# Branch B of the attention computed with v as the weights and its result left transposed

## The reference

```python
sc = jnp.einsum('bqhd,bqkd->bhqk', q_blk, k_g).astype(jnp.float32) * scale
dist = jnp.abs(t[None, :, None] - top_idx).astype(jnp.float32)
sc = sc - slopes[None, :, None, None] * dist[:, None]
sc = jnp.where(valid[:, None], sc, -jnp.inf)
p = jax.nn.softmax(sc, axis=-1)
return jnp.einsum('bhqk,bqkd->bqhd', p.astype(v.dtype), v_g)
...
merged = g_a * (y_a @ w_branch_a[l]) + g_b * (y_b @ w_branch_b[l])
h = h + merged @ w_out[l]
```

## Time and profile before

| | us |
|---|---|
| median of 3 runs | 1095.45 (1093.77 to 1096.46) |
| the profiled execution, its own time | 1092.93 |
| its span | 1091.1 |
| PE busy | 1000.3 (92%) |
| DVE busy | 508.9 (47%) |
| ACT busy | 318.3 (29%) |

### The profile page before, as it was taken

The page is one execution under the profiler, slowest core; times in us unless marked ns, Lnnn a source line. Parts: engine busy times, 40 slices in busy tenths (PEclk is TensorE's granted clock), DMA queues, the critical chain, the costliest instruction groups (busy, mean ns, idle before and its releaser), DMA issues.

```text
span 1091.1 us, 12310 instructions
## 1 busy us (share of the span) xinstructions
PE 1000.3 (92%) x4817; PEld 632.3 (58%) x4817; DVE 508.9 (47%) x917; ACT 318.3 (29%) x588; POOL 38.1 (3%) x58
## 2 busy tenths in 40 slices
PE   4999989999999999999998499999999998998994
PEld 3777866677878889787767234444443333343342
DVE  4234799979536534523335623333333323333235
ACT  6332346565553335533223111111111100100113
POOL 1000000000000000000000110000000000000000
PEclk9999999999999999999999699999999999999997
DMA  6522222111232434512277699999999999999991
GB/s 189 164 78 77 81 74 69 48 39 40 77 117 77 134 99 139 187 61 77 78 261 287 256 422 428 425 428 426 426 426 428 425 428 426 427 426 427 427 393 79
DMA packets 63917, 261.21 MB, mean 239 GB/s; under 512 B 11201, under 2 KB 38898, under 8 KB 49778
## 3 DMA queue, kind: packets, MB, share of 16 engines
q1 hardware_dynamic: 59442, 248.60, 57.6%
q0 software_dynamic: 3104, 7.35, 1.9%
q10 hardware_dynamic: 1312, 4.46, 1.1%
HBM read 260.12 MB, written 4.19 MB: 242 GB/s over the span
## 4 chain that ended last, share of the span: by engine, by line
PE 73%; DMA 13%; DVE 9%; issue 3%; ACT 2%; DVEq 0%; ACTq 0%; POOLq 0%
PE ps L1826 16%; PE ps L1564 12%; DMA eraw<-in_w 12%; PE ps L1566 11%; PE ps L1565 11%; PE ps L1852 8%; PE ps L1863 2%; PE ps L1864 2%; PE ps L1726 2%; PE ps L1755 1%; PE ps L1777 1%; PE ps L1705 1%; DVE nmax L1208 1%; DVE wlo L1153 1%; DVE s L1206 1%
## 5 line engine op out<-in xcount | busy, mean ns | idle before, releaser
L1826 PE MATMUL ps<-eraw,XT 128*64 128x512 f32 x1024 | 234.5, 601 | 12.4 <-DMA eraw<-in_w 11.6
L1153 DVE TENSOR_TENSOR wlo<-raw,whi 128x2048 fp32r<-128x2048 f32 (+2 forms) x43 | 95.9, 2230 | 138.9 <-ACT whi L863 138.9
L1826 PEld LDWEIGHTS ps<-eraw,XT 128*64 128x64 f32 x1024 | 70.2, 137 | 138.6 <-issue 134.7
L1852 PE MATMUL ps<-eraw,HT 128*64 128x512 f32 x512 | 113.0, 593 | 9.0 <-issue 8.1
L1439 DVE TENSOR_TENSOR h<-ps,h 128x512 f32<-128x512 f32 x128 | 79.4, 682 | 83.4 <-PE ps L1864 83.4
L1564 PE MATMUL ps<-xT_hi,whi 128*128 128x512 f32 (+1 forms) x256 | 105.3, 411 | 0.0
L1565 PE MATMUL ps<-xT_lo,whi 128*128 128x512 f32 (+1 forms) x256 | 100.6, 393 | 0.0
L1566 PE MATMUL ps<-xT_hi,wlo 128*128 128x512 f32 (+1 forms) x256 | 100.6, 393 | 0.0
L863 ACT ACTIVATE whi<-raw 128x2048 fp32r<-128x2048 f32 (+2 forms) x43 | 80.1, 1863 | 55.9 <-PE ps L1566 54.0
L1852 PEld LDWEIGHTS ps<-eraw,HT 128*64 128x64 f32 x512 | 39.5, 137 | 80.5 <-issue 80.5
L1010 ACT ACTIVATE HT<-ps 128x512 f32<-128x512 f32 x16 | 9.6, 598 | 215.4 <-PE ps L1837 215.4
(11 more groups left out here) (301 smaller groups left out, 1544.0 us busy)
## 6 DMA issues: line engine op xcount, KB each, us to landing
eraw<-in_w SPq DMA_DIRECT2D x82, 2048.0 KB, 29.1
eraw<-in_w SPq DMA_DIRECT2D x28, 1024.0 KB, 11.2
raw<-in_w_in SPq DMA_DIRECT2D x9, 1024.0 KB, 5.2
raw<-in_w_gate SPq DMA_DIRECT2D x8, 1024.0 KB, 5.7
raw<-in_w_ckv SPq DMA_DIRECT2D x8, 1024.0 KB, 5.7
raw<-in_w_out SPq DMA_DIRECT2D x4, 1024.0 KB, 5.2
raw<-in_w_cq SPq DMA_DIRECT2D x4, 1024.0 KB, 5.1
raw<-in_w_co SPq DMA_DIRECT2D x4, 1024.0 KB, 5.1
```

The source lines that it names most:

```text
L1153: dve.tensor_tensor(wlo[n % 2][:, 0:w], raw[n % RING][:, 0:w], whi[n % 2][:, 0:w].bitcast(f32), ALU.subtract).then_inc(w_lo, 1)
L1826: ins = pe.matmul(ps[1 + c // 2][rows, :], XT[p % 2][:, kk, rows], eraw[slot][:, first + 512 * k:first + 512 * k + 512], start=(kk == 0), ...
L1852: ins = pe.matmul(ps[4 + n][rows, :], HT[:, ff, rows], eraw[slot][:, first + D * f + 512 * n:first + D * f + 512 * n + 512], start=(ff == ...
```

## The change

The exponentials of a unit of branch B are divided by their sums before they are turned: DVE still inverts the sums, and ACT then scales both heads' rows in place (two new activations, L941 of the changed kernel). The turned rows are then the moving side and v (128 x 64) the weights. Head m of the pair lands in the partitions 64 m to 64 m + 63 of the bank, so the result comes out turned, with the heads one under the other. ACT copies it to `ybT_hi` and DVE subtracts into `ybT_lo`, 128 x 128 in each unit. `yb`, its 16 transposes and the eight 512-column copies behind unit 31 are gone. `ybT_lo` takes the place where `yb` was, which `h` overwrites later, and so the load of `h` is moved behind the last merge and behind `mrow`.

```diff
-    ybT_lo = at("ybT_lo", [P, 4, SEQ], f32r, R_C, 24 * KB)
+    ybT_lo = at("ybT_lo", [P, 4, SEQ], f32r, R_H, 8 * KB)
...
-    steps += [("yT", "b", j) for j in range(4)] + [("split", CH_G[-1] + 2)] + [("sigmoid", i) for i in range(KT // 2)]
+    steps += [("split", CH_G[-1] + 2)] + [("sigmoid", i) for i in range(KT // 2)]
...
-            b, n = use[("yT", "b", 3)]
-            pool.wait_ge(bank_free[b], n + 1)
-            pool.dma_start(h[:, :, :], x[0].rearrange("(t p) n -> p t n", p=P)).then_inc(h_loaded, 16)
             pool.wait_ge(mg_low, len(MERGES))
             pool.dma_start(mrow[:, :, :], mem[0].rearrange("(t p) n -> p t n", p=P)).then_inc(mem_loaded, 16)
+            pool.dma_start(h[:, :, :], x[0].rearrange("(t p) n -> p t n", p=P)).then_inc(h_loaded, 16)
...
+                elif kind == "fin" and UNITS[s[1]][0] == "B":
+                    u = s[1]
+                    qt = UNITS[u][1]
+                    act.wait_ge(sum_inverted, u - len(A_UNITS) + 1)
+                    for m in (0, 1):
+                        b = sbuf[u % 3][m][:, 0:kv(qt)]
+                        ins = act.activation(b, b, ACT.Copy, scale=rsum[:, u % 3, m:m + 1])
+                    ins.then_inc(fin_done, 1)
...
+                    else:
+                        act.activation(ybT_hi[:, j, P * qt:P * qt + P], tile_of(*s)[:, 0:P], ACT.Copy).then_inc(act_hi, 1)
...
                     for g in (2 * s[1], KT + 2 * s[1]):
+                        copied("fm", CH_G[g // 2], 1)
...
-                        dve.reciprocal(rsum[:, u % 3, 0:2], ssum[:, u % 3, 0:2]).then_inc(fin_done, 1)
-                        dve.wait_ge(fin_done, u + 1)
+
+                        dve.reciprocal(rsum[:, u % 3, 0:2], ssum[:, u % 3, 0:2]).then_inc(sum_inverted, 1)
...
-                        p = tile_of(*s)[:, 0:2 * DH_B].rearrange("p (m n) -> p m n", m=2)
-                        dve.tensor_tensor(yb[:, qt, P * j:P * j + P].rearrange("p (m n) -> p m n", m=2), p,
-                                          rsum[:, u % 3, 0:2].unsqueeze(2).to_broadcast([P, 2, DH_B]),
-                                          ALU.mult).then_inc(freed(*s), 1)
+                        c = slice(P * qt, P * qt + P)
+                        dve.wait_ge(act_hi, T_NO[s])
+                        dve.tensor_tensor(ybT_lo[:, j, c], tile_of(*s)[:, 0:P], ybT_hi[:, j, c].bitcast(f32),
+                                          ALU.subtract).then_inc(freed(*s), 1)
...
-                        for k in range(qt + 1):
-                            v = va[:, k, P * j:P * j + P] if br == "A" else vb[:, k, :]
-                            ins = pe.matmul(o[:, DH_B * m:DH_B * m + (P if br == "A" else DH_B)], pT[u % 2][m][:, k, :], v,
+                    for k in range(qt + 1):
+                        if br == "A":
+                            ins = pe.matmul(o[:, 0:P], pT[u % 2][0][:, k, :], va[:, k, P * j:P * j + P],
                                             start=(k == 0), stop=(k == qt))
+                        else:
+
+                            for m in (0, 1):
+                                ins = pe.matmul(o[DH_B * m:DH_B * m + DH_B, 0:P], vb[:, k, :], pT[u % 2][m][:, k, :],
+                                                start=(k == 0), stop=(k == qt))
...
-                        for br in "ba":
-                            for jj in range(4):
-                                copied("yT", br, jj)
+                        for jj in range(4):
+                            copied("yT", "a", jj)
+                        copied("av", len(UNITS) - 1)
```

More of the change, by code:

```diff
@@ L124, in build @@
     ya = at("ya", [P, TT, 512], f32, R_H)
-    yb = at("yb", [P, TT, 512], f32, R_H, 8 * KB)
     h = at("h", [P, TT, D], f32, R_H)
@@ L476, in build @@
     max_done, exp_done, fin_done = sem("max_done"), sem("exp_done"), sem("fin_done")
+    sum_inverted = sem("sum_inverted")
     sig_done, mg_sum, mg_high, mg_low = sem("sig_done"), sem("mg_sum"), sem("mg_high"), sem("mg_low")
@@ L507, in build @@
     for s in steps:
-        if s[0] in ("xT", "yT", "mT", "cT"):
+        if s[0] in ("xT", "yT", "mT", "cT") or s[0] == "av" and UNITS[s[1]][0] == "B":
             T_NO[s] = len(T_NO) + 1
@@ L873, in _ @@
                 elif kind == "yT":
[L874 to L879, removed]
+                    j = s[2]
+                    act.activation(yaT_hi[:, j, :], tile_of(*s)[:, :], ACT.Copy, scale=cols[:, 40:41]).then_inc(act_hi, 1)
                 elif kind == "fT":
@@ L1162, in _ @@
                 elif kind == "yT":
-                    br, j = s[1:]
+                    j = s[2]
                     dve.wait_ge(act_hi, T_NO[s])
[L1165 to L1170, removed]
+                    dve.scalar_tensor_tensor(yaT_lo[:, j, :], tile_of(*s)[:, :], cols[:, 40:41],
+                                             yaT_hi[:, j, :].bitcast(f32), ALU.mult, ALU.subtract).then_inc(freed(*s), 1)
                 elif kind == "index":
@@ L1613, in _ @@
                 elif kind == "yT":
-                    br, j = s[1:]
-                    if s == ("yT", "b", 0):
-                        copied("av", len(UNITS) - 1)
+                    j = s[2]
                     if s == ("yT", "a", 0):
@@ L1620, in _ @@
                     for t in range(TT):
-                        ins = pe.transpose(o[:, P * t:P * t + P], (ya if br == "a" else yb)[:, t, P * j:P * j + P], ident[:, :])
+                        ins = pe.transpose(o[:, P * t:P * t + P], ya[:, t, P * j:P * j + P], ident[:, :])
                     ins.then_inc(full(*s), 1)
```

## The result

The changed kernel takes 1101.16 us (median of 20 runs, 1094.88 to 1102.7); the kernel before took 1095.67 in the same rounds (20 runs, 1093.59 to 1096.55). By the medians it is slower by 5.5 us. The ratio of the mean times is 1.0044 (1.0032 to 1.0056), so the loss is small but clear of no change. The time lies within the range of the prediction, 5.2 above the number.

A forecast was written before the change was run, and what follows sets the result against it. PE was taken to bound the kernel (busy 92%), with DVE just behind in branch B. Branch B +6.1, its end -5.5 and `h` 0 gave +0.6 on 1092.93, 1093.5; the median's 2.5 offset made it 1096, range 1088 to 1103.

The forecast's parts named there:

- The end of the branch: From branch B's last product to the merges: transposes, copies and the slow clock go, gaining 5.5 us, or 3.8 if slow.
- The products: Products with v in branch B: sixteen take 1.10 us instead of 1.72, a gain only where PE sets the pace.
- The second rival: Ring costs and half-array products do not pay, staying at 0.108 each plus switches: 4.8 us more, 1101; chance 0.34 with neighbours.
- The ring: Branch B: ACT's scalings wait for DVE's reciprocals, DVE for ACT's copies, delaying later reciprocals; branch 6.1 us longer.
- the walk: Following DVE's reciprocals unit by unit through branch B: unit 20 at 244.6, unit 26 at 283.1, 10.2 us late.
- The first rival: PE sets the pace throughout branch B, ACT having slack: gain 10.2 us, median 1085; chance 0.24 with its neighbours.
- The step that failed: Units 17 to 20 of branch B: PE 1.7 us late in unit 18, reciprocal of 20 at 244.6, 2.0 late.
- the likeliest sum: Whole kernel: branch B +6.1, its end -5.5, load of `h` 0, together +0.6 us; called same, chance 0.42.
- The load of `h`: Moved behind `mrow`, it was to stay hidden ahead of PE's need near 383.3: cost 0, bound +1 us.
- the cover of 4.6: The 4.6 us margin before PE needs the weight split behind `mrow`; `mrow` might come 5.5 later, exceeding it by 1.1.
- the forecast's own: The range given to the likeliest case alone, about no change: 1093 to 1099 us.
- the full range: 1088 to 1103 us: low is most of the first rival, high the second rival with one slow-clock hole.

The follow-up runs named there:

- the spare matmuls: The changed kernel with 4 and 11 extra 512-column matmuls ahead of PE's waits in units 18 and 20, output unchanged: 1099.49 us (before 1094.76).
- the second profile: The changed kernel run and profiled once more with no edit: 1099.85 us in one run (before 1095.4).
- the norm later: The changed kernel with ACT's scalings behind the exponentials and the norm of `ya` one unit later: 1091.71 us (before 1094.76).

## Why the prediction was off by its number

**The end of the branch: right.** Forecast a hole of 0.8 and the full clock; measured 0.93 and the full clock. The gain of 5.5 stands, less 0.1. The clock stayed up behind this last hole in all ten profiles that have the new end (0.90 to 0.93). But the reason given, a hole much shorter than 2.26, is weaker than it reads: the clock also stayed up behind a hole of 2.25 at this place, where before had only the scaling added, and it fell behind 0.86 and 1.01 in unit 18. In part this step was luck.

**The products: right.** Forecast 1.10 for sixteen, with the cost of entering the mode; measured 1.03 from start to start of the next work, and 0.09 ahead of it (0.32 from 319.78 to 320.10, for 0.23 between full products). The Trainium skill, TensorEngine Tiling (Array Packing), Key Properties, says that a change of mode drains the engine; the trace agrees, if the time beyond the records is the drain, and it is small. Eight records take 0.59 and sixteen 1.03 until the next work, so a record takes 0.055 and 0.15 comes behind them, with the 0.09 ahead. The second rival's ground, halves that do not pay, is therefore wrong, though its time of 1101 is the one that came out.

**The ring: right in kind, and nearly in size.** From the reciprocal of 20 to that of 26 the walk gave 38.5; measured 39.1, and each of the six steps is within 0.2. The pairs of scalings are a part of the rest: one of 256 columns holds ACT for 0.82, where 0.7 was taken (253.63 to 254.45). Behind the last wait for the gate copy the forecast was 31.5 to the end of the last product; measured 31.5 (289.68 to 321.19). That it fits so well is luck, for two errors of 0.4 cancel: half of the turn of unit 26 was done before (287.91), and the units behind it give back 2.9 instead of 3.3, the longest 0.56 each (4.81 for 5.37) instead of 0.62. The first rival, ACT with slack because it is busy for 11.23 of 20 us, fell: the ring set the pace though ACT was busy for 13.62 and DVE for 14.48 of 20.

**The step that failed** is "with unit 18 and the norm of `ya` behind it, the reciprocal of 20 comes at 244.6". The walk took each instruction of PE at full clock. It had forecast PE late by 1.7 in unit 18 and did not ask what idle times of that size do to the clock. Behind them it fell in unit 18: 12 matmuls, nearly all at the lower level, took 2.4 us more, and the reciprocal came 2.9 late. The text priced such a fall at 1.65 "where PE then sets the pace", for the holes over 2.26 alone, and left it out of the likeliest sum. In a ring a fall can cost also where PE does not set the pace, when DVE waits for PE's product, as in unit 18; in unit 20, where DVE was busy with `wlo` meanwhile, it cost 0.1. Where no fall came in unit 18, the reciprocal of 20 was the forecast one: 244.39 with the spare matmuls, 244.28 with `ybT_hi` on DVE. With a fall half as long, in the second profile, it came 1.5 less late. The merges' lag of 4.3 against the 0.6 forecast is then 2.9 for the fall in unit 18, 0.6 from the reciprocal of 20 to that of 26, and 0.3 behind it. This says where the lag arose, not what one would save by keeping the clock up: the spare matmuls saved 0.3, since the clock then fell at 261.

**The load of `h`: right**, hidden by 2.3 us. (The sum behind its bound slips: 5.5 is 0.9 over the cover of 4.6, not 1.1.)

**The range.** 1101.16 lies outside the forecast's own 1093 to 1099. It lies inside the full range only because of the second rival, whose ground, halves that do not pay, the runs refuted; that is luck.

**What is left.** The medians differ by 5.5, of which the branch explains 4.3. The rest is in shared code, where the clock fell more often in the profile of after than in that of before. The 20 times of the changed kernel lie in two groups, 4 at 1094.9 to 1096.5 with a mean clock of 0.973 to 0.975, and 16 at 1100.8 to 1102.7 with 0.965 to 0.969. The profiles of after (1101.53) and of the spare matmuls (1095.42), one of each size, differ by falls in shared code. That the groups of the unprofiled runs differ in the same way is argued from their clocks, not shown, and the second profile, 1099.85 at a mean clock of 0.973, fits neither group. Why the clock falls more often in most executions of the changed kernel stays open; nothing tried here moved these falls by themselves.

## What to carry to other kernels

A wait in an in-order queue costs all that stands behind it and all who wait for that, so price a moved operation by walking the ring through its unit, not by its duration or the busy shares; then put it behind whatever others wait for. Here two steps further back in the list, and the norm one unit later, turned 5.5 us lost into 8.0 won, with the same instructions; the norm alone is worth 3.5 of them. When such a walk forecasts holes on PE, even of about 1 us, walk it a second time with the matmuls behind them at the lower clock, and take both times as bounds: here such holes brought a fall in some profiles and none in others.

## What the runs showed of the hardware

- The clock fell behind two idle times of 0.86 and 1.01 with 0.33 us of work between them, in the changed kernel's first profile (0.85 and 1.01 in its second), and behind 0.95 and 1.01 where before had only the scaling added. With 1.19 and 1.01 at the same place it did not (the copy on DVE). Behind 2.26 ahead of the merges it fell at once in the kernel before, 1.3 us later in the same kernel with the norm moved, and not at all behind 2.25 where before had only the scaling added. A hole of about 3.05 ahead of a turn of `ya` brought a fall with the spare matmuls, and none (1.00 from 250 to 270 us) with the norm later. So the length of one hole does not decide.
- A stretch at the lower clock made the ring 2.9 us later in unit 18, where DVE waited for the copy of PE's product, and 0.1 in unit 20, where DVE was busy meanwhile. In shared code one fall cost about 1.6.
- The same shared code, in executions whose merges start within 0.3 us, took 771.9 and 777.7 us.
- Products with 64-column weights in the two halves of the array and 128 moving columns take 0.055 us each and 0.15 once behind them, against 0.108 for 128-column weights and 64 moving ones.
- A copy with a scale for each row on ACT costs little itself: 0.69 for a pair of 128 columns and 0.91 for a pair of 256, next to waits of up to 3.7 us, 16.6 in all, ahead of the pairs.
